# Decay rows of the delta rule through DRAM instead of TensorE transposes, and small loads issued ahead of the first square root

## The reference

```python
h = rms_norm(x, g_mix)
proj = h @ w_in                       # q, k, v, z, beta, a | q, k, v of the attention | two gates
qkv = silu(causal_depthwise_conv(concat(qa, ka, va), conv_w))
beta = sigmoid(beta_in)
g = -exp(a_log) * softplus(a_in + dt_bias)          # (tokens, 8 heads)
# gated delta rule, per head: gc is the running sum of g over the tokens of a chunk
decay[i, j] = exp(gc[i] - gc[j]) for i >= j, else 0
A = strict_lower((beta * k) @ k.T * decay); T = inverse(I + A)
o = (q @ k.T * decay) @ (T @ ...) + ...
# differential softmax attention with a T5 relative-position bias, rel_bias (32 buckets, 8 heads)
# lambda = exp(sum(lambda_q1*lambda_k1)) - exp(sum(lambda_q2*lambda_k2)) + 0.2
x = x + (sigmoid(gate_a) * oa + sigmoid(gate_b) * od) @ w_o
x = x + top-4-of-32 expert FFN(rms_norm(x))         # w_up 1024x2048, w_down 1024x1024 per expert
```

## Time and profile before

| | us |
|---|---|
| median of 3 runs | 1350.95 (1349.63 to 1358.93) |
| the profiled execution | 1349.63 |
| its span in the profile | 1347.6 |
| PE busy | 1253.5 (93%) |
| DVE busy | 370.1 (27%) |
| ACT busy | 255.0 (19%) |
| POOL busy | 63.6 (5%) |

### The profile page before, as it was taken

How to read it: one execution, slowest core, us unless ns; L and a number is a source line. 1 busy time by engine, 2 the same in 40 slices (tenths; PEclk the granted TensorE clock), 3 DMA queues, 4 the chain that set the end, 5 groups by cost and what they waited for, 6 DMA issues and landing times.

```text
span 1347.6 us, 14033 instructions
## 1 busy us (share of the span) xinstructions
PE 1253.5 (93%) x5565; PEld 542.0 (40%) x5565; DVE 370.1 (27%) x891; ACT 255.0 (19%) x517; POOL 63.6 (5%) x104
## 2 busy tenths in 40 slices
PE   6989999978998999999999999989999998999997
PEld 5878456634443333333333333323333332333332
DVE  4586734554413121121112111111211111121111
ACT  2441021355121111111111111111111111111110
POOL 5160200001000000000000000000000000000000
PEclk9999999988997999999999999999999999999999
DMA  8642533113298999999999999999999999999995
GB/s 259 144 165 84 170 109 125 63 62 119 69 398 333 429 428 427 427 427 427 427 427 427 428 427 428 428 428 427 427 427 428 427 427 428 427 428 427 428 427 216
DMA packets 57403, 452.71 MB, mean 336 GB/s; under 512 B 10713, under 2 KB 10857, under 8 KB 32673
## 3 DMA queue, kind: packets, MB, share of 16 engines
q1 hardware_dynamic: 53536, 447.76, 80.0%
q0 software_dynamic: 1488, 3.85, 1.7%
q10 hardware_dynamic: 2320, 0.26, 0.2%
HBM read 448.69 MB, written 3.15 MB: 335 GB/s over the span
## 4 chain that ended last, share of the span: by engine, by line
PE 56%; DMA 33%; DVE 7%; ACT 2%; issue 2%; SPq 0%; DVEq 0%; ACTq 0%
DMA ring<-in_w_up_dram 32%; PE pb L1420 15%; PE pb L1456 11%; PE pb L1166 7%; PE pb L1147 5%; PE pb L1375 3%; PE pb L1389 3%; PE pb L1308 2%; PE pb L1135 2%; PE pb L1381 1%; PE pb L1439 1%; DMA ring<-in_w_in_dram 1%; DVE ring L877 1%; DVE ring L876 1%; DVE ring L787 1%
## 5 line engine op out<-in xcount | busy, mean ns | idle before, releaser
L1420 PE MATMUL pb<-ring,buf_a 128*64 128x512 f32 x2048 | 456.0, 596 | 44.6 <-DMA ring<-in_w_up_dram 44.6
L1420 PEld LDWEIGHTS pb<-ring,buf_a 128*64 128x64 f32 x2048 | 143.5, 137 | 339.2 <-issue 246.6
L1456 PE MATMUL pb<-ring,buf_b 128*64 128x512 f32 x1024 | 226.8, 595 | 0.0
L1098 DVE TENSOR_SCALAR buf_a<-pb 128x512 f32<-128x512 f32 x32 | 22.1, 692 | 673.8 <-PE pb L1420 673.8
L1166 PE MATMUL pb<-ring,hT 128*128 128x512 f32 x384 | 176.6, 607 | 0.9 <-PE pb L1166 0.6
L1456 PEld LDWEIGHTS pb<-ring,buf_b 128*64 128x64 f32 x1024 | 70.7, 137 | 131.8 <-issue 127.9
L724 ACT ACTIVATE buf_a<-buf_a 128x512 f32<-128x512 f32 x32 | 20.1, 630 | 471.9 <-DVE buf_a L1098 471.9
L1166 PEld LDWEIGHTS pb<-ring,hT 128*128 128x128 f32 x384 | 71.2, 194 | 81.3 <-issue 80.7
L1147 PE MATMUL pb<-hT,ring 128*128 128x256 f32 x384 | 91.3, 393 | 2.0 <-DMA ring<-in_w_in_dram 2.0
L1147 PEld LDWEIGHTS pb<-hT,ring 128*128 128x128 f32 x384 | 74.0, 196 | 12.3 <-issue 2.4
L1375 PE MATMUL pb<-xt,buf_c 128*64 128x512 f32 x264 | 65.7, 619 | 1.0 <-DVE buf_c L1043 1.0
(11 more groups left out here) (274 smaller groups left out, 823.0 us busy)
## 6 DMA issues: line engine op xcount, KB each, us to landing
ring<-in_w_up_dram SPq DMA_DIRECT2D x128, 2048.0 KB, 41.1
ring<-in_w_down_dram SPq DMA_DIRECT2D x64, 2048.0 KB, 43.4
ring<-in_w_in_dram SPq DMA_DIRECT2D x18, 2048.0 KB, 7.9
ring<-in_w_o_dram SPq DMA_DIRECT2D x2, 2048.0 KB, 8.6
t_rows<-ring POOLq DMA_DIRECT2D x1, 1536.0 KB, 34.8
xt<-in_x_dram SPq DMA_DIRECT2D x2, 512.0 KB, 4.5
ring<-t_rows POOLq DMA_DIRECT2D x1, 1024.0 KB, 6.1
out_dram<-xt SPq DMA_DIRECT2D x2, 512.0 KB, 2.7
```

Of the source, the lines that this page charges most:

```text
L1420: ins = mm(pb[64 * hf:64 * hf + 64, n_, :], xg[:, c, :], slot(s)[:, at_:at_ + 512], start=False, stop=(c == KC - 1), skip_group_check=True)
L1456: ins = mm(pb[64 * hf:64 * hf + 64, 2, :], actT[:, j, hf_in, :], slot(s)[:, at_:at_ + 512], start=(c == 0), stop=(c == KC - 1), skip_group ...
```

## The change

1. In `extra` the step `ba` moves from tile 2 to tile 1, `gc` from 4 to 3, and `E` from 8 to 9. The step `gr` goes, with PE's 16 transposes and the view `psG`. A step `gl` comes in after tile 6.
2. In `gc` ACT now also stores `gc`, transposed element by element, to a new DRAM tensor `gc_dram` of 16 rows of 128. In `gl` ACT waits for that store and starts a load that broadcasts the 16 rows, 8 KB, to all 128 partitions of `EP` (1 MB).
3. In `E` DVE waits for that load in place of PE's transposes, and its 17 instructions read `EP` in SBUF, in place, where they read PSUM. DVE's wait for `s_const` at this place and PE's wait for `s_dif` ahead of the first `kq` go.
4. ACT's eight loads are issued ahead of the square root of the start, with `rel_bias` first and `wba` second.

```diff
--- before.py
+++ after.py
@@ -107,7 +107,7 @@
     put(40, ("oan",))
 
     sched = []
-    extra = {2: [("ba",)], 4: [("gc",)], 5: [("gr",)], 8: [("E",)], 12: [("nr", 0)], 19: [("kq", 0, 0)], 20: [("kq", 0, 1)],
+    extra = {1: [("ba",)], 3: [("gc",)], 6: [("gl",)], 9: [("E",)], 12: [("nr", 0)], 19: [("kq", 0, 0)], 20: [("kq", 0, 1)],
              21: [("kq", 1, 0)], 22: [("kq", 1, 1)]}
     for t in range(24):
         sched.append(("tile", t))
@@ -210,9 +210,9 @@
         psA2 = pb[:, 2:4, :].rearrange("p b (h s j) -> p (b h) s j", h=2, s=2)
         psA_f = pb[:, 2:4, :].rearrange("p b j -> p (b j)")
         psB = pb[:, 4:6, :].rearrange("p b (h j) -> p (b h) j", h=4)
-        psG = pb[:, 2:6, :].rearrange("p b (h j) -> p (b h) j", h=4)
 
         r_dram = nc.dram_tensor("t5_rows", [8, P, 384], F32)
+        gc_dram = nc.dram_tensor("gc_rows", [16, P], F32)
         m_dram = nc.dram_tensor("m_blocks", [64, 1024], F32)
         t_dram = nc.dram_tensor("t_blocks", [64, 1024], F32)
 
@@ -278,7 +278,7 @@
         s_conv, s_sig, s_silu = sem("conv_done"), sem("conv_sigmoid_done"), sem("silu_done")
         s_sq, s_nmm = sem("norm_squares_ready"), sem("norm_sums_done")
         s_bap, s_bact, s_bdve = sem("beta_a_projected"), sem("beta_a_act_steps"), sem("beta_a_dve_steps")
-        s_ug, s_gcp, s_gc, s_grow = sem("g_ready"), sem("gc_summed"), sem("gc_ready"), sem("gc_rows_turned")
+        s_ug, s_gcp, s_gc, s_gcst, s_gcl = sem("g_ready"), sem("gc_summed"), sem("gc_ready"), sem("gc_stored"), sem("gc_rows_loaded")
         s_kdd, s_kda, s_dif, s_dex = sem("kdec_difference"), sem("kdec_ready"), sem("decay_difference"), sem("decay_ready")
         s_psA, s_psAf = sem("psA_steps_done"), sem("psA_steps_taken")
         s_psB, s_psBf = sem("psB_steps_done"), sem("psB_steps_taken")
@@ -540,13 +540,13 @@
                 act_e.wait_ge(s_var, ROOTS.index(name) + 1)
                 sc.activation(y, w, ACT.Sqrt).then_inc(s_root, 1)
 
-            root("x", rr, rt2)
+            act_e.dma_start(rowbuf[:, 384:384 + NBUCK], rel_bias.rearrange("b h -> h b")).then_inc(s_rbld, 16)
             act_e.dma_start(wba[:, :, :], win[:, C_BA:C_BA + 2 * H].rearrange("(k p) n -> p k n", p=P)).then_inc(s_wba, 16)
-            act_e.dma_start(rowbuf[:, 384:384 + NBUCK], rel_bias.rearrange("b h -> h b")).then_inc(s_rbld, 16)
             act_e.dma_start(dtb, dt_bias[0:1, :].to_broadcast([P, H])).then_inc(s_small, 16)
             act_e.dma_start(alog, a_log[0:1, :].to_broadcast([P, H])).then_inc(s_small, 16)
             for i, src in enumerate((lambda_q1, lambda_k1, lambda_q2, lambda_k2)):
                 act_e.dma_start(lamrow[:, i, :], src[0:1, :].to_broadcast([P, 64])).then_inc(s_lamld, 16)
+            root("x", rr, rt2)
 
             def tok2(ap):
                 return ap.rearrange("p (b j) -> p b j", b=2)
@@ -595,7 +595,11 @@
                     sc.activation(lamv[:, 0:2], lamv[:, 0:2], ACT.Exp).then_inc(s_lam, 1)
                 elif it[0] == "gc":
                     act_e.wait_ge(s_gc, 1)
+                    act_e.dma_start(bass.AP(gc_dram, 0, [[1, P], [P, 16]]), gc.rearrange("p b h -> p (b h)")).then_inc(s_gcst, 16)
                     sc.activation(egc, gc, ACT.Exp).then_inc(s_bact, 1)
+                elif it[0] == "gl":
+                    act_e.wait_ge(s_gcst, 16)
+                    act_e.dma_start(ring[:, 1, 2 * D:], bass.AP(gc_dram, 0, [[0, P], [1, 2 * D]])).then_inc(s_gcl, 16)
                 elif it[0] == "E":
                     act_e.wait_ge(s_kdd, 1)
                     sc.activation(kdec, kdec, ACT.Exp).then_inc(s_kda, 1)
@@ -832,13 +836,12 @@
                     dve.wait_ge(s_bact, 3)
                     dve.wait_ge(s_gc, 1)
                     v.tensor_scalar(negc, egc[:, 1, :], -1.0, None, ALU.mult)
-                    dve.wait_ge(s_grow, 1)
-                    dve.wait_ge(s_const, 1)
-                    link(v.tensor_tensor(kdec, psG[:, 0:H, P - 1], gc[:, 0, :], ALU.subtract))
+                    dve.wait_ge(s_gcl, 16)
+                    link(v.tensor_tensor(kdec, EP[:, 0, :, P - 1], gc[:, 0, :], ALU.subtract))
                     dve.sem_inc(s_kdd, 1)
                     for b in range(NB):
                         for h in range(H):
-                            ins = v.scalar_tensor_tensor(out=EP[:, b, h], in0=psG[:, b * H + h], scalar=gc[:, b, h:h + 1], in1=negm, op0=ALU.subtract, op1=ALU.add)
+                            ins = v.scalar_tensor_tensor(out=EP[:, b, h], in0=EP[:, b, h], scalar=gc[:, b, h:h + 1], in1=negm, op0=ALU.subtract, op1=ALU.add)
                         ins.then_inc(s_dif, 1)
                 elif it == ("nr", 0):
                     dve.wait_ge(s_nmm, 8)
@@ -1190,17 +1193,10 @@
                     for b in range(NB):
                         ins = mm(pb[:, 6, 416 + 8 * b:424 + 8 * b], tri, gg[:, b, :], start=True, stop=True)
                     ins.then_inc(s_gcp, 1)
-                elif it[0] == "gr":
-                    pe.wait_ge(s_gc, 1)
-                    for b in range(NB):
-                        for h in range(H):
-                            ins = nc.tensor.transpose(psG[:, b * H + h], gc[:, b, h:h + 1].to_broadcast([P, P]), ident)
-                    ins.then_inc(s_grow, 1)
                 elif it[0] == "kq":
                     _, b, hf = it
                     startA(it)
                     if b == 0 and hf == 0:
-                        pe.wait_ge(s_dif, NB)
                         pe.wait_ge(s_silu, 16)
                     for i in range(4):
                         h = 4 * hf + i
```

## The result

The changed kernel takes 1367.6 us (median of 4 runs, 1364.7 to 1368.6) against 1353.4 before (4 runs, 1349.6 to 1358.9): a ratio of 1.0103, with a 95% interval of 1.0081 to 1.0125, some 14 us slower. The time forecast was 1366, so the number holds. The way to it was another. Of the 15.5 us that the forecast sums, 12.2 were the lambda vectors' (15.5 less the 3.3 of rival B), and these came in time; most of the loss stands where part 5 of the prediction wrote "hidden", at the trip of `gc` through DRAM. That was rival A, with sizes of its own.

A forecast was written before the change was run, and what follows sets the result against it. Ahead of the DMA-bound expert loop, the tile stage's delay was to come out one for one: +17.4 us, holding the late start and earlier `ba`, less 1.9 for transposes, is +15.5 on 1349.6; with 1.3 for the median, 1366 us, range 1351 to 1376.

The forecast's parts named there:

- rival B: Tile stage: no DMA wait lasts, so only parts 1 to 3 are left, +3.3 us, 1354; chance 0.18.
- part 5: Trip of `gc` through DRAM: store starts at 58, ends at 68, ACT asks at about 71, so no cost.
- rival A: `t_rows` on the other eight engines: lambdas at 29, `gc` store late, ACT stands at `gl`; about +9, 1360; chance 0.22.
- Part 1: Start of the kernel: eight loads ahead of the square root put the first tile at 24.8, +8.3 us.
- Part 2: `ba` one tile earlier: ACT's and DVE's turns no longer meet POOL's cast, giving back 3.1 of 8.3 us.
- Part 3: PE's 16 transposes go, -1.9 us; DVE's instructions reading SBUF keep 0.27 us each.
- Part 4: `rel_bias` first: `t_rows` starts earlier, lambdas wait beside it until about 50 us, tile 5 ends 17.4 us later.
- Part 6: POOL's chain against DVE: meets tiles 5 to 9 instead of 9 to 13; same loss, 0, 3 us either way.

The follow-up runs named there:

- all loads ahead: The kernel before with only its eight small loads ahead of the root and `rel_bias` first; ratio 1.0059 to the kernel before.
- root first: The changed kernel with the root ahead of its eight loads again and `wba` ahead of `rel_bias`; ratio 1.0113 to the kernel before.
- `t_rows` held back: The changed kernel with POOL's store of `t_rows` waiting until `gl`'s load has landed; ratio 1.0057 to the kernel before.
- lambdas late: The changed kernel with its four lambda loads moved from the start into ACT's step of `ba`; ratio 1.0239 to the kernel before.
- `gl` late: The changed kernel with `gl` behind tile 11 and `E` behind tile 14; ratio 1.0029 to the kernel before, 0.9999 with the root also ahead of the loads.
- the 16 rows: The changed kernel with `gc` turned once on PE and stored as 16 rows of 512 B; ratio 1.0060 to the kernel before.

## Why the prediction was right in its number and wrong in its way

**Part 1** (first tile at 24.8): 24.73. Right, and the root at 18.6 for 18.7. The 12.70 that was taken as fixed was 12.17.

**Part 2** (3.1 back): nearly. With no lambda wait, tile 5 was to end at 51.9 and ends at 49.86 + 3.70 = 53.6. What lacks is a term the prediction hadn't: the first tile's matmuls run at half pace behind PE's idle start. The window of 24 to 28 us of the changed kernel, then the same one of "all loads ahead", then 32 to 36 us of root first (length, busy us by engine, PE's granted clock, DMA share, GB/s):

```profile
24.00:28.00 4.00, 3.27 (x8) 2.65 (x9) 0.67 (x1) 0.00 (x0) 3.71 (x3) 1.00 1.05 368
```

```profile
24.00:28.00 4.00, 3.22 (x16) 2.61 (x15) 0.84 (x2) 0.00 (x0) 3.71 (x3) 1.00 1.07 358
```

```profile
32.00:36.00 4.00, 4.00 (x10) 3.12 (x10) 3.23 (x10) 1.28 (x2) 2.40 (x2) 0.50 0.44 45
```

The price in the changed kernel is 2.4 us (9.56 for 7.15), and what `t_rows` held back shows without it, +2.0 at tile 6, is near rival B's. So but for the clock part 2 was about right. Rival B's sum, 8.3 - 3.1 - 1.9 = +3.3, becomes 5.1 at tile 6 with it.

**Part 3** (-1.9): the transposes are gone; DVE's 16 reads from SBUF take 0.27 us each, as from PSUM.

**Part 4, the step that failed:** "at 24.3 it still had 249 packets to move; their rate halves there". POOL did move at 16.4 (16.6), and its store started at 22.4 (22.6 forecast). But the first packet came at 27, not 24.3. The 1.7 us from start to first packet were an estimate that left out what was queued ahead; they are right for the kernel before (28.98 to 30.73), and 4.6 went by here, until the packets queued ahead had run down. In lambdas late, whose queue from ACT is empty by 24 us, it is 4.6 as well, so that SP's pieces are the ones that count. And the turns of rows 9 were read as a rule for any queue beside `t_rows`, while they are the end of a story: in rows 8, just ahead, SP's queue has no row at all, with 1.0 of a piece's 2 MB moved. Whoever comes behind waits first, and gets turns later; whoever is ahead goes through. The lambdas were ahead. Moved behind, they land at 57.9, and that kernel is 32 us slower than the one before, 18 more than the changed kernel.

**Part 5, the second step that failed:** "hidden". It hung on part 4, since the store was to start at 58, when `t_rows` ends. It started at 47.7. Rival A foresaw just that (46.5) and what follows: ACT standing at `gl` from 57 (58.5), PE stopping behind tile 8 (so). It was undersized: the store's end at 67 to 72 was 75.2, tile 9 at 70 to 74 was 77.5, and "2 to 4 us come back" didn't happen; `E` cost 4.7 us of idle and a slow tile on top. +9 was +18 in the trace. The turns were counted right (1029 packets in 15 us on 8 engines are 0.12 us each), but from 58.5 on, and they began at about 60.

**Part 6:** POOL's first subtraction ran while DVE idled; its cast and copy met DVE once (76.41, 4.77 us for three steps that take 1.52 together elsewhere), and `E`'s 16 steps met nothing (4.29 us).

**The sum** was right by luck: two errors cancelled, 12.2 for lambdas that cost nothing, against 0 for a wait that costs 11.8 between tile 6 (+5.1) and tile 9 (+16.9). The two share a cause, the place of a transfer relative to `t_rows`, so in this kernel one stood in for the other (lambdas late shows that a kernel can have late lambdas, too), and the rival should have been given the same care as the forecast. Its chance of 0.22 was too low: ACT's queue moved 165 packets per us in rows 6 and 44 in rows 7, so its drain was in sight.

By the runs, the 14 us are about 10 for the wait at `gl` (1.0103 to 1.0029) and 4 for the late start (1.0029 to 0.9999, two intervals that overlap), taken out in this order. In the other order the start is worth nothing and the wait all of it (1.0113 to 0.9999). The late start is 8.2 us at tile 0 against the kernel before, and 6.5 between the two kernels with `gl` late; of these, 4.2 are left at tile 4, as the one with the early start loses the rest at `ba`.

Left open: why a transfer waits on a filled engine for many packets and then alternates (rows 8 and 9, root first); the packets' counts show that it does, no run shows what holds it. No run takes away SP's piece of weights, started ahead of the store, so that its part in the changed kernel's wait from 57 to 60 us isn't known. And `E` and POOL's subtractions were moved together with `gl`, so that their price apart isn't known to better than some 3 us.

## What to carry to other kernels

Ask of each small DMA which large one is ahead of it on the same engines: behind a long store that fills its engines, a few KB took 10.5 to 31.5 us here. Put the wait for such a trip where the trip has surely ended, and don't let an engine with per-tile work stand in it. A DMA start can hold its sequencer for microseconds (5.42 for the third small load here), so what the first tile needs goes ahead of loads that nobody needs yet.

## What the runs showed of the hardware that was not expected

- A new transfer beside a long one goes in two parts: first on the free engines, and on the filled ones after a stand of 5 to 10 us, in turns with the long one if that still runs. It shows for 4-byte elements (1032 and 1029 packets), for 16 rows (16 and 16), and, in the kernel before, for a piece of weights, started at 34.2 us. 36 to 42 us of the kernel before (none of q1 follows from 42 to 48, rows 8):

```profile
q1 hardware_dynamic: 505, 1.02, 44.1%
```

- With `t_rows` held back, 2048 elements of 4 bytes pass in under 4 us (48.1 to 51.8), but the store counts as landed only 5 us after its last packet. The Trainium skill (DMA: Bandwidth & Descriptors, Anatomy of one DMA) puts most of a DMA's fixed 2 us, on GpSimd's path, on the receipt of the write. ACT's stores here show no such fixed time: 5.2 us in this kernel, 0.4 in the changed one (last packet at 74.7, landed at 75.16), 0.7 for the 16 rows.
- A start, not only a transfer, can stand there: three of ACT's small loads took 3.7 to 4.3 us each to start beside `t_rows`, while the store of `gc` took 0.39.
- PE's first tiles ran at 1.2 or at 2.4 GHz by whether the granted clock had risen ahead of them: the first two take 9.56 us in the changed kernel, 7.15 at full pace. The window's clock column reads 1.00 where the trace has no record of the clock, so that the matmuls' own pace is what to go by at a kernel's start.
